# Spacing the rows of h 2112 bytes apart and the weight slots 4112 bytes apart in a one-core fp32 transformer kernel

## The chip, the core and the metric

The kernel runs on one NeuronCore of a Trainium2 chip. The core has a matrix engine (PE, with its own queue of weight loads, PEld), a vector engine (DVE), a scalar engine (ACT), a general engine (POOL) and a queue engine that only issues transfers (SP). Its on-chip memory (SBUF) has 128 partitions; a tensor such as `[128, 8, 512]` of fp32 lies in every partition as 8 rows of 512 numbers, 2048 bytes each, one behind the other. Matmul results go to a second memory, `ps`, of 8 banks per partition. The metric is device time in microseconds (us) of one execution of the whole program; lower is better.

## What is computed

A two-layer hybrid block for a latent diffusion model. There are 256 latent tokens and 256 context tokens (512 columns in the kernel), model width 1024. Each layer is a half-step SwiGLU, a token mixer and another half-step SwiGLU:

```
def ffn_sublayer(s, m, g_norm, w_in, w_out):
    h = modulate(rmsnorm(s, g_norm), m[0], m[1])
    return s + FFN_RES * m[2] * swiglu(h, w_in, w_out)

def mixer_sublayer(...):                       # cut
    h = modulate(rmsnorm(s, p["norm_mix"]), m[0], m[1])
    pool, qkv, z, ba, aq, ak, av, gate = split_cols(h @ p["w_in"])
    # multi-scale pooling | bidirectional gated DeltaNet (chunks of 64) | GQA with 2-D rotary
    m = ga * (y_pool @ wa) + gb * (y_dn @ wb) + gc * (y_att @ wc)
    x = x + mx[2] * (m @ w_out)
```

All in fp32. D_FF is 2816, so one SwiGLU multiplies by a 1024 x 5632 matrix and then a 2816 x 1024 one; the mixer's input projection is 1024 x 5136. The last mixer and the last SwiGLU need only the 256 latent tokens. The modulations come from SiLU(c) times a 1024 x 9216 matrix per layer, and a last RMSNorm gives the output.

## The kernel before

**Tiles and products.** Activations lie with channels on the partitions and tokens in the columns: `x[:, k, :]` is channel block k (128 channels) of all 512 tokens. The weights come in blocks of 128 output channels, `[128, 1024]` for a sum over eight channel blocks. To keep fp32 accuracy each operand is split into a rounded upper part and a rest, both in a one-pass fp32 format (`F32R`): `h` into `h_hi` and `h_lo`, a weight block into `w_hi` and `w_lo`. `products` (lines 2031 to 2037) issues three matmuls per pair of tiles: upper weights by upper rows, upper weights by lower rows, lower weights by upper rows. Each has its own weight load of 128 x 128 and streams 512 columns (both token halves), or 256.

**What the rows and slots are.** `h_hi` and `h_lo` hold the normed activations, eight rows k, written once per stage by ACT (`h_hi`) and DVE (`h_lo`) and then read by every matmul of the stage's first product. The hidden activations of a SwiGLU and the merged branches go to `a_hi` and `a_lo`, 22 rows of 512 numbers each. Weights go through a ring of four slots (`RING = 4`): a transfer lands in `raw[:, j, :]`, ACT rounds it to `w_hi[:, j, :]` (`cast`, line 825), and DVE subtracts (`lower`, line 1449) to give `w_lo[:, j, :]`. `raw` and `w_lo` are the same bytes: `raw` is allocated and released, and `w_lo` is placed over it. In the same way `gate_in` (24,576 bytes) lies over `h_hi` and the start of `h_lo`, and is used when h is done.

**Order.** The work is written out by hand per engine, with semaphores. SP issues the load of weight block b when the matmuls of block b - 4 are done (`load`, line 588); ACT casts when it has landed; DVE lowers when it is cast; PE waits for `s_lo` of that block. POOL issues the transfers of the modulation weights (`ada`), and DVE multiplies them in between (line 1481). The stages are SwiGLU, mixer, SwiGLU, SwiGLU, mixer, SwiGLU. In the long parts the loops have PE run block after block, 24 matmuls each.

**Where the tensors lie.** Within a partition they are placed one behind the other in the order of the declarations, each start rounded up to a multiple of 32 bytes. With the pad of 8 numbers ahead of it (`pad_rows`), `x` starts at a multiple of 2048 bytes, and so do, in turn, `h_hi`, `h_lo`, `raw`/`w_lo`, `w_hi`, `ada`, `buf_a`, `buf_b`, `a_hi` and `a_lo`. Hence every row of h and of a starts at a multiple of 2048 bytes and every weight tile of 128 numbers at a multiple of 512 bytes. The second half of a row (the context tokens) starts 1024 bytes behind. Not everything lies so: in the mixer `pre` takes 4160 bytes, so `conv`, `kT`, `pool_mats`, `prob` and others behind it start 64 bytes past a multiple of 2048.

Of the kernel before, what the change touches and what calls it, by code (L numbers as in the profile page):

```python
# [8 lines left out]
F32R = mybir.dt.float32r  # L9
# [4 lines left out]
P = 128  # L14
D = 1024
KD = D // P
LAT, CTX = 256, 256
TOK = LAT + CTX
# [23 lines left out]
MIX_STAGE = (1, 4)  # L42
STAGE_BASE = (FFN_BASE[0], MIX_BASE[0], FFN_BASE[1], FFN_BASE[2], MIX_BASE[1], FFN_BASE[3])
RING = 4
SPLIT_STAGES = (1, 2, 3, 4)
NORM_PARTS = (1, 2, 2, 2, 2, 1, 1)
SPLIT_OUT = 5
# [79 lines left out]
def build_program(nc, a):  # L127
    with ExitStack() as ctx:
        def sb(name, shape, dt=F32, at=ctx):
            return at.enter_context(nc.sbuf_tensor(name, shape, dt))  # L130
# [25 lines left out]
        x = sb("x", [P, KD, TOK])  # L156
        with ExitStack() as s:
            gate_in = sb("gate_in", [P, 4, 3, TOK], at=s)
        h_hi = sb("h_hi", [P, KD, TOK], F32R)
        h_lo = sb("h_lo", [P, KD, TOK], F32R)  # L160
        with ExitStack() as s:
            raw = sb("raw", [P, RING, KD * P], at=s)
        w_lo = sb("w_lo", [P, RING, KD * P], F32R)
        w_hi = sb("w_hi", [P, RING, KD * P], F32R)
        ada = sb("ada", [P, 2, KD * P])
        buf_a = sb("buf_a", [P, 2, TOK])
        buf_b = sb("buf_b", [P, 2, TOK])
# [55 lines left out]
        s = ExitStack()  # L223
# [16 lines left out]
        s = ExitStack()  # L240
# [98 lines left out]
        ps = ctx.enter_context(nc.psum_tensor("ps", [P, 8, 512], F32))  # L339
# [1615 lines left out]
        def _(pe):  # L1955
# [203 lines left out]
            def mixer_pe(l):  # L2159
# [12 lines left out]
                pe.wait_ge(bal.sem, bal.at(l, 1))  # L2172
                for k in range(KD):
                    wh, wl = ba_hi[:, k * P:(k + 1) * P], ba_lo[:, k * P:(k + 1) * P]
                    pe.matmul(ps[:, 6, :], wh, h_hi[:, k, :], start=(k == 0), stop=False)
                    pe.matmul(ps[:, 6, :], wh, h_lo[:, k, :], start=False, stop=False)
                    ins = pe.matmul(ps[:, 6, :], wl, h_hi[:, k, :], start=False, stop=(k == KD - 1))
                ins.then_inc(bap.sem, 1)
                for n in range(RING, N_PROJ):

# [3 lines left out]
                    if 9 <= n < 12:  # L2184
                        m = n - 2
                        pe.wait_ge(evac.sem, evac.at(l, m + 1))
                        for t in range((TOK if m == 7 else no) // P):
                            ins = pe.transpose(ps[:, m - 5, t * P:(t + 1) * P],
                                               channel_rows(m)[:, t * P:(t + 1) * P], ident)
                        ins.then_inc(tkt.sem, 1)  # L2190
                    if n == 6:
                        pe.wait_ge(bat.sem, bat.at(l, 1))
                        for t in range(TT):
                            ins = pe.transpose(ps[:, 6, t * 16:(t + 1) * 16], ba_rowsT[0:16, t * P:(t + 1) * P],
                                               ident[0:16, 0:16])
# [56 lines left out]
                for s in range(no // LAT):  # L2252
                    if s:
                        pe.wait_ge(pl2.sem, pl2.at(l, s))
                    for g in range(4):
                        r = slice((g % 2) * HD, (g % 2 + 1) * HD)
                        for kt in range(2):
                            ins = pe.matmul(ps[r, 4, (g // 2) * LAT:(g // 2 + 1) * LAT],
                                            pool_nat[:, 2 * s + kt, g * HD:(g + 1) * HD], pool_mats[:, kt, g, :],
                                            start=(kt == 0), stop=(kt == 1))  # L2260
# [5 lines left out]
                    for g in range(4):  # L2266
                        r = slice((g % 2) * HD, (g % 2 + 1) * HD)
                        ins = pe.matmul(ps[r, 5, (g // 2) * LAT:(g // 2 + 1) * LAT], w_pool[r, g // 2, :],
                                        pooled[r, s, g // 2, :], start=True, stop=True)
# [54 lines left out]
                for j in range(4):  # L2324
# [3 lines left out]
                    for t in range(TT):  # L2328
                        ins = pe.transpose(ps[:, j % 2, t * P:(t + 1) * P], src[:, t * P:(t + 1) * P], ident)
# [3 lines left out]
                for d in range(2):  # L2333
                    ins = pe.matmul(ps[:, 5, d * TT * 4:(d + 1) * TT * 4], tri(d), gdt[:, :, 4 * d:4 * d + 4],
                                    start=True, stop=True)
                for d in range(2):
                    ins = pe.matmul(ps[:, 5, 32 + d * TT * 4:32 + (d + 1) * TT * 4], ones[:, :], gdt[:, :, 4 * d:4 * d + 4],
                                    start=True, stop=True)
# [3 lines left out]
                for w in range(2):  # L2342
# [26 lines left out]
                    for t in (0, 2):  # L2369
                        for q in range(4):  # L2370
# [3 lines left out]
                            ins = pe.matmul(ps[:, 4 + q % 2, cols], qkvT[r, 2 + w, cols], qkvT[r, 2 + w, cols],  # L2374
                                            start=True, stop=True)
                            if l == 0 or t == 0:
                                ins = pe.matmul(ps[:, q % 2, cols], qkvT[r, 2 + w, cols], qkvT[r, w, cols],
                                                start=True, stop=True)
# [16 lines left out]
                    for i, b in enumerate(LEVELS):  # L2395
                        for h in range(2):
                            if i:
                                pe.wait_ge(tup.sem, tup.at(l, 2 * NL * w + 2 * (i - 1) + h + 1))
                            for d in range(2):
                                for q in range(4):  # L2400
                                    ins = pe.transpose(t_bank(d, h)[:, q, :], t_mat(d, 4 * h + q), ident)  # L2401
                            ins.then_inc(trp.sem, 1)
                            for q in range(4):
                                ins = pe.matmul(x_bank(h)[:, :, q, :].rearrange("p z (i c) -> p z i c", c=b),  # L2404
                                                amT[:, 4 * h + q, :], t_old(b, 4 * h + q, 1), start=True, stop=True)
                            ins.then_inc(xps.sem, 1)
                        for h in range(2):
# [3 lines left out]
                            for q in range(4):  # L2411
                                ins = pe.matmul(x_bank(h)[:, :, q, :], um[:, 4 * h + q, :], x_half(h)[:, :, q, :],  # L2412
                                                start=True, stop=True)
                            ins.then_inc(yps.sem, 1)
                    for h in range(2):
                        pe.wait_ge(tup.sem, tup.at(l, 2 * NL * (w + 1) - 1 + h))
                        for d in range(2):
                            for q in range(4):
                                ins = pe.transpose(t_bank(d, h)[:, q, :], t_mat(d, 4 * h + q), ident)
                            ins.then_inc(fin.sem, 1)  # L2420
                    for d in range(2):
                        pe.wait_ge(uev.sem, uev.at(l, 4 * w + 3 + d))
                        for q in range(8):
                            h = 2 * w + q % 2
                            ins = pe.matmul(ps[:, d, q * HD:(q + 1) * HD], u_mat(d)[:, q, :],
                                            vd_nat[:, q // 2, h * HD:(h + 1) * HD], start=True, stop=True)
                        ins.then_inc(ups.sem, 1)
                    pe.wait_ge(keg.sem, keg.at(l, w + 1))
                    for d in range(2):
                        for q in range(8):  # L2430
                            r = slice((q % 2) * HD, (q % 2 + 1) * HD)
                            ins = pe.matmul(ps[r, 2 + d, (q // 2) * P:(q // 2 + 1) * P], ke[:, 8 * d + q, :],
                                            u_mat(d)[:, q, :], start=True, stop=True)
# [232 lines left out]
```

## Time and profile before

| | |
|---|---|
| runs | 2300.62, 2301.11, 2306.16 us; median 2301.11 |
| profiled execution | 2311.86 us, of which 2310.2 us from the first to the last instruction (the span) |
| mean granted clock of PE | 0.975 of 2.4 GHz |
| PE busy | 2213.9 us, 96% of the span, 12654 matmuls |
| PE's weight loads | 1863.6 us, beside the matmuls |
| DVE busy | 1370.2 us, 59% |
| ACT busy | 885.3 us, 38% |
| POOL busy | 218.7 us, 9% |
| transfers | 303.86 MB, mean 132 GB/s |

An engine's busy time is the sum of its instructions' durations with overlaps counted once; a matmul's duration overlaps the next one's, since they are pipelined, so the pace of PE is read from the distances between starts, not from the durations. The profiled execution is 0.5% longer than the median of the runs; the three runs lie 5.5 us apart.

### The profile page before, as it was taken

Reading aid. Unit: us, or ns where it says so; the run is one execution under the profiler, and the core shown is the slowest. Engines: PE = TensorE matmul, PEld = TensorE weight load, DVE = VectorE, ACT = ScalarE, POOL = GpSimd, SP = SyncE. Lnnn points to the kernel's source line nnn. Section 1 sums busy time; section 2 is a strip of 40 time slices with the busy share of each in tenths; the row PEclk is TensorE's granted clock in tenths of the full one; section 3 lists DMA queues with packets and bytes.
Section 4 is the critical chain, followed back from the end, with each engine's and each line's share of the span. In section 5 each row is a group of like instructions: output and inputs, shape, how many; then the busy total and the mean of one; then the engine's idle time right before and its main releaser. Section 6 shows DMA issues by size and latency. Waiting matters only on the chain.

```text
span 2310.2 us, 33776 instructions
## 1 busy us (share of the span) xinstructions
PE 2213.9 (96%) x12654; PEld 1863.6 (81%) x12654; DVE 1370.2 (59%) x2301; ACT 885.3 (38%) x1375; POOL 218.7 (9%) x287
## 2 busy tenths in 40 slices
PE   6999999999999999999999999999999998898998
PEld 3788878987558777888888888888889777788998
DVE  4787876634456447478875356555356555665554
ACT  2433322533444325343222243332235543455553
POOL 0001022000001200300011100000210001001001
PEclk8999999999999989999999999999999999899999
DMA  6455554323012205345554334444343311144555
GB/s 261 146 197 185 197 182 135 133 82 93 31 42 69 70 27 200 109 164 191 199 189 130 95 121 148 138 153 130 106 130 118 109 46 49 66 163 146 182 173 155
DMA packets 96913, 303.86 MB, mean 132 GB/s; under 512 B 10673, under 2 KB 17329, under 8 KB 95921
## 3 DMA queue, kind: packets, MB, share of 16 engines
q1 hardware_dynamic: 77520, 232.96, 31.0%
q0 software_dynamic: 18720, 69.21, 8.9%
q8 instruction: 68, 1.11, 0.2%
q10 hardware_dynamic: 576, 0.34, 0.0%
q14 instruction: 29, 0.23, 0.0%
HBM read 291.99 MB, written 10.49 MB: 131 GB/s over the span
## 4 chain that ended last, share of the span: by engine, by line
PE 56%; DVE 4%; ACT 2%; issue 1%; DMA 1%; DVEq 0%; ACTq 0%; SPq 0%
PE ps L2035 17%; PE ps L2036 16%; PE ps L2037 16%; DVE w_lo L1449 1%; PE ps L2286 1%; PE ps L2307 1%; PE ps L2401 1%; PE ps L2473 1%; PE ps L2404 1%; PE ps L2471 1%; PE ps L2412 1%; PE ps L2223 0%; PE ps L2295 0%; ACT w_hi L825 0%; DMA raw<-in_w_up 0%
## 5 line engine op out<-in xcount | busy, mean ns | idle before, releaser
L2035 PE MATMUL ps<-h_hi,w_hi 128*128 128x512 f32 (+1 forms) x2176 | 779.9, 358 | 30.8 <-DVE w_lo L1449 12.7
L2036 PE MATMUL ps<-h_lo,w_hi 128*128 128x512 f32 (+1 forms) x2176 | 761.7, 350 | 0.0
L2037 PE MATMUL ps<-h_hi,w_lo 128*128 128x512 f32 (+1 forms) x2176 | 761.2, 350 | 0.0
L1449 DVE TENSOR_TENSOR w_lo<-raw,w_hi 128x1024 fp32r<-128x1024 f32 (+2 forms) x416 | 475.3, 1146 | 462.8 <-ACT w_hi L825 458.0
L825 ACT ACTIVATE w_hi<-raw 128x1024 fp32r<-128x1024 f32 (+2 forms) x416 | 404.6, 974 | 613.5 <-DMA raw<-in_w_down 306.7
L2035 PEld LDWEIGHTS ps<-h_hi,w_hi 128*128 128x128 f32 x2176 | 419.1, 193 | 121.1 <-issue 43.0
L2037 PEld LDWEIGHTS ps<-h_hi,w_lo 128*128 128x128 f32 x2176 | 419.1, 193 | 52.1
L2036 PEld LDWEIGHTS ps<-h_lo,w_hi 128*128 128x128 f32 x2176 | 419.7, 193 | 48.9
L2035 PE MATMUL ps<-a_hi,w_hi 128*128 128x512 f32 (+1 forms) x1050 | 359.4, 342 | 9.4 <-DVE buf_b L1912 3.7
L2036 PE MATMUL ps<-a_lo,w_hi 128*128 128x512 f32 (+1 forms) x1050 | 357.2, 340 | 0.0
L2037 PE MATMUL ps<-a_hi,w_lo 128*128 128x512 f32 (+1 forms) x1050 | 357.0, 340 | 0.0
L1481 DVE CUSTOM_DVE_ANT_0 ps<-ada,c_wide 128x1024 f32<-128x1024 f32 x256 | 319.2, 1247 | 6.8 <-DMA ada<-in_w_ada_t 1.6
L2035 PEld LDWEIGHTS ps<-a_hi,w_hi 128*128 128x128 f32 x1050 | 199.0, 189 | 35.7 <-DVE buf_b L1912 5.9
L2037 PEld LDWEIGHTS ps<-a_hi,w_lo 128*128 128x128 f32 x1050 | 199.0, 190 | 22.2
L2036 PEld LDWEIGHTS ps<-a_lo,w_hi 128*128 128x128 f32 x1050 | 199.1, 190 | 21.9
L723 POOL DMA_DIRECT2D ada<-in_w_ada_t x128 | 67.9, 531 | 804.1 <-DVE ada_sum L1481 797.2
L944 ACT ACTIVATE a_hi<-buf_b 128x512 f32 (+3 forms) x88 | 51.0, 579 | 201.3 <-DVE buf_b L1467 201.3
L1472 DVE TENSOR_TENSOR a_lo<-buf_b,a_hi 128x512 f32 (+3 forms) x88 | 54.7, 622 | 26.2 <-ACT a_hi L944 26.1
L685 POOL TENSOR_TENSOR buf_a<-x 128x512 f32<-128x512 f32 (+1 forms) x34 | 44.8, 1317 | 239.5 <-DVE x L1455 239.2
L1455 DVE SCALAR_TENSOR_TENSOR x<-ps,mod,x 128x256 f32<-128x256 f32 (+1 forms) x68 | 30.4, 479 | 53.6 <-PE ps L2037 53.6
L1467 DVE TENSOR_TENSOR buf_b<-buf_a,ps 128x512 f32<-128x512 f32 (+1 forms) x88 | 54.0, 614 | 8.4 <-PE ps L2037 8.4
L940 ACT ACTIVATE buf_a<-ps 128x512 f32<-128x512 f32 (+1 forms) x88 | 47.3, 537 | 14.2 <-PE ps L2037 13.8
(259 smaller groups left out, 1829.2 us busy)
## 6 DMA issues: line engine op xcount, KB each, us to landing
raw<-in_w_up SPq DMA_DIRECT2D x176, 512.0 KB, 3.7
ada<-in_w_ada_t POOLq DMA_DIRECT2D x128, 512.0 KB, 3.8
raw<-in_w_down SPq DMA_DIRECT2D x64, 384.0 KB, 3.1
raw<-in_w_gate SPq DMA_DIRECT2D x48, 512.0 KB, 3.5
raw<-in_w_down SPq DMA_DIRECT2D x64, 320.0 KB, 2.9
raw<-in_w_proj SPq DMA_DIRECT2D x32, 512.0 KB, 3.4
raw<-in_w_merge SPq DMA_DIRECT2D x16, 512.0 KB, 3.7
raw<-in_w_out SPq DMA_DIRECT2D x16, 512.0 KB, 3.3
```

The costliest lines, as they stand in the source:

```text
L685: link(pool.tensor_tensor(buf_a[:, 1, 0:n], xk, xk, ALU.mult))
L723: pool.dma_start(ada[:, j, :], a["w_ada_t"][ADA_FIRST - KD + 2 * r + j]).then_inc(s_ada[j], 16)
L825: return act.activation(w_hi[:, j % RING, 0:cols], raw[:, j, 0:cols], ACT.Copy)
L940: act.activation(buf_a[:, j, 0:n], ps[:, 2 * j, 0:n], ACT.Silu).then_inc(s_silu, 1)
L944: act.activation(a_hi[:, q, 0:n], buf_b[:, j, 0:n], ACT.Copy).then_inc(s_ahi, 1)
L1449: vec.tensor_tensor(w_lo[:, j % RING, 0:cols], raw[:, j, 0:cols], w_hi[:, j % RING, 0:cols].bitcast(F32), ALU.subtract).then_inc(s_lo, 1)
L1467: vec.tensor_tensor(buf_b[:, j, 0:n], buf_a[:, j, 0:n], ps[:, 2 * j + 1, 0:n], ALU.mult).then_inc(s_mul, 1)
L1472: vec.tensor_tensor(a_lo[:, q, 0:n], buf_b[:, j, 0:n], a_hi[:, q, 0:n].bitcast(F32), ALU.subtract).then_inc(s_alo, 1)
L1481: vec.tensor_tensor_reduce(ps[:, 6:8, :].rearrange("p b n -> p (b n)"), ada[:, j, :], c_wide[:, i, :], 1.0, 0.0, ALU.mult, ALU.add, ada_su ...
L2035: pe.matmul(out, wh, rows_hi[:, i, c], start=first, stop=False)
L2036: pe.matmul(out, wh, rows_lo[:, i, c], start=False, stop=False)
L2037: return pe.matmul(out, wl, rows_hi[:, i, c], start=False, stop=last)
```

## The change

Each row of `h_hi` and `h_lo` gets 16 unused numbers (64 bytes) behind its 512, and each ring slot of `raw`, `w_lo` and `w_hi` gets 4 unused numbers (16 bytes) behind its 1024. The three matmuls that took a whole row by `:` now name its 512 columns. Everything else is as it was, and every engine's list of instructions has the same operations on the same shapes in the same order; only addresses differ.

```
--- before.py
+++ after.py
@@ -42,6 +42,7 @@
 MIX_STAGE = (1, 4)
 STAGE_BASE = (FFN_BASE[0], MIX_BASE[0], FFN_BASE[1], FFN_BASE[2], MIX_BASE[1], FFN_BASE[3])
 RING = 4
+H_GAP, W_GAP = 16, 4
 SPLIT_STAGES = (1, 2, 3, 4)
 NORM_PARTS = (1, 2, 2, 2, 2, 1, 1)
 SPLIT_OUT = 5
@@ -156,12 +157,12 @@
         x = sb("x", [P, KD, TOK])
         with ExitStack() as s:
             gate_in = sb("gate_in", [P, 4, 3, TOK], at=s)
-        h_hi = sb("h_hi", [P, KD, TOK], F32R)
-        h_lo = sb("h_lo", [P, KD, TOK], F32R)
+        h_hi = sb("h_hi", [P, KD, TOK + H_GAP], F32R)
+        h_lo = sb("h_lo", [P, KD, TOK + H_GAP], F32R)
         with ExitStack() as s:
-            raw = sb("raw", [P, RING, KD * P], at=s)
-        w_lo = sb("w_lo", [P, RING, KD * P], F32R)
-        w_hi = sb("w_hi", [P, RING, KD * P], F32R)
+            raw = sb("raw", [P, RING, KD * P + W_GAP], at=s)
+        w_lo = sb("w_lo", [P, RING, KD * P + W_GAP], F32R)
+        w_hi = sb("w_hi", [P, RING, KD * P + W_GAP], F32R)
         ada = sb("ada", [P, 2, KD * P])
         buf_a = sb("buf_a", [P, 2, TOK])
         buf_b = sb("buf_b", [P, 2, TOK])
@@ -2172,9 +2173,9 @@
                 pe.wait_ge(bal.sem, bal.at(l, 1))
                 for k in range(KD):
                     wh, wl = ba_hi[:, k * P:(k + 1) * P], ba_lo[:, k * P:(k + 1) * P]
-                    pe.matmul(ps[:, 6, :], wh, h_hi[:, k, :], start=(k == 0), stop=False)
-                    pe.matmul(ps[:, 6, :], wh, h_lo[:, k, :], start=False, stop=False)
-                    ins = pe.matmul(ps[:, 6, :], wl, h_hi[:, k, :], start=False, stop=(k == KD - 1))
+                    pe.matmul(ps[:, 6, :], wh, h_hi[:, k, 0:TOK], start=(k == 0), stop=False)
+                    pe.matmul(ps[:, 6, :], wh, h_lo[:, k, 0:TOK], start=False, stop=False)
+                    ins = pe.matmul(ps[:, 6, :], wl, h_hi[:, k, 0:TOK], start=False, stop=(k == KD - 1))
                 ins.then_inc(bap.sem, 1)
                 for n in range(RING, N_PROJ):
```

What the addresses become, from the declarations (bytes within a partition, modulo 2048):

| tensor | start before | start after | its rows or slots after |
|---|---|---|---|
| x | 0 | 0 | unchanged |
| h_hi | 0 | 0 | row k at 64k |
| h_lo | 0 | 512 | row k at 512 + 64k |
| raw, w_lo | 0 | 1024 | slot j at 1024 + 16j |
| w_hi | 0 | 1088 | slot j at 1088 + 16j |
| ada, buf_a, buf_b, a_hi, a_lo | 0 | 1152 | rows and slots still 2048 or 4096 apart |
| what lies behind them | s | s + 1152 | distances among them unchanged |

The rows of `a_hi` and `a_lo` keep their spacing of 2048 bytes, but they too now start at another offset than the weight tiles that they are multiplied by. The tensors end 1152 bytes later and still fit.

## Rows read from the trace of the kernel before

**Rows 1.** The page: busy time by engine, the slices and the granted clock.

```profile
PE 2213.9 (96%) x12654; PEld 1863.6 (81%) x12654; DVE 1370.2 (59%) x2301; ACT 885.3 (38%) x1375; POOL 218.7 (9%) x287
PE   6999999999999999999999999999999998898998
PEclk8999999999999989999999999999999999899999
```

**Rows 2.** PE's waits by what released it: in total, times, longest.

```profile
PE ps L2401 <- ACT tm L1213: 19.1, 4, 8.4
PE ps L2035 <- DVE w_lo L1449: 15.8, 14, 4.4
PE ps L2035 <- DVE h_lo L1357: 9.8, 6, 3.4
PE ps L2035 <- DVE h_lo L1409: 6.0, 5, 1.5
```

**Rows 3.** PE in order of time, 512 columns, rows of h: start, duration.

```profile
1099.79 0.39 PE L2035 MATMUL ps<-h_hi,w_hi 128*128 128x512 f32 x1
1100.02 0.39 PE L2036 MATMUL ps<-h_lo,w_hi 128*128 128x512 f32 x1
...
1105.91 0.39 PE L2035 MATMUL ps<-h_hi,w_hi 128*128 128x512 f32 x1
```

**Rows 4.** The same, 512 columns, rows of a.

```profile
300.57 0.39 PE L2035 MATMUL ps<-a_hi,w_hi 128*128 128x512 f32 x1
...
303.97 0.39 PE L2035 MATMUL ps<-a_hi,w_hi 128*128 128x512 f32 x1
```

**Rows 5.** The same, 256 columns, rows of h, last SwiGLU.

```profile
2149.77 0.28 PE L2036 MATMUL ps<-h_lo,w_hi 128*128 128x256 f32 x1
...
2153.13 0.28 PE L2037 MATMUL ps<-h_hi,w_lo 128*128 128x256 f32 x1
```

**Rows 6.** Costliest groups with shapes apart: busy us, mean ns, idle before.

```profile
L2036 PE MATMUL ps<-h_lo,w_hi 128*128 128x512 f32 x1296 | 507.5, 392 | 0.0
L2036 PEld LDWEIGHTS ps<-h_lo,w_hi 128*128 128x128 f32 x2176 | 419.7, 193 | 48.9
L1449 DVE TENSOR_TENSOR w_lo<-raw,w_hi 128x1024 fp32r<-128x1024 f32 x288 | 353.5, 1229 | 301.3 <-ACT w_hi L825 297.2 <-DVE mod_rest L1486 2.2
L825 ACT ACTIVATE w_hi<-raw 128x1024 fp32r<-128x1024 f32 x288 | 303.2, 1055 | 306.8 <-DMA raw<-in_w_up 275.9 <-DMA raw<-in_w_out 28.2 <-DMA raw<-in_w_merge 2.1
L2036 PE MATMUL ps<-a_lo,w_hi 128*128 128x512 f32 x566 | 220.3, 389 | 0.0
L2036 PEld LDWEIGHTS ps<-a_lo,w_hi 128*128 128x128 f32 x1050 | 199.1, 190 | 21.9
```

**Rows 7.** Two stretches, engines busy (instructions), clock, DMA share, GB/s.

```profile
1360.00:1540.00 180.00, 180.00 (x859) 151.79 (x858) 107.16 (x154) 72.46 (x90) 8.47 (x16) 1.00 0.44 143
2150.00:2300.00 150.00, 150.00 (x1251) 149.90 (x1250) 81.06 (x100) 73.58 (x99) 11.50 (x13) 1.00 0.57 174
```

**Rows 8.** Transfers, whole span: count, KB each, median us to landing.

```profile
raw<-in_w_up SPq DMA_DIRECT2D x176, 512.0 KB, 3.7
masks<-in_consts SPq DMA_DIRECT2D x2, 1024.0 KB, 5.7
pool_mats<-in_pool_mats SPq DMA_DIRECT2D x2, 1024.0 KB, 4.9
```

**Rows 9.** Transfers, from 2050 to 2300 us.

```profile
raw<-in_w_up SPq DMA_DIRECT2D x44, 512.0 KB, 3.3
```

More of the change, by code:

```diff
@@ L44 @@
 RING = 4
+H_GAP, W_GAP = 16, 4
 SPLIT_STAGES = (1, 2, 3, 4)
@@ L158, in build_program @@
             gate_in = sb("gate_in", [P, 4, 3, TOK], at=s)
-        h_hi = sb("h_hi", [P, KD, TOK], F32R)
-        h_lo = sb("h_lo", [P, KD, TOK], F32R)
+        h_hi = sb("h_hi", [P, KD, TOK + H_GAP], F32R)
+        h_lo = sb("h_lo", [P, KD, TOK + H_GAP], F32R)
         with ExitStack() as s:
-            raw = sb("raw", [P, RING, KD * P], at=s)
-        w_lo = sb("w_lo", [P, RING, KD * P], F32R)
-        w_hi = sb("w_hi", [P, RING, KD * P], F32R)
+            raw = sb("raw", [P, RING, KD * P + W_GAP], at=s)
+        w_lo = sb("w_lo", [P, RING, KD * P + W_GAP], F32R)
+        w_hi = sb("w_hi", [P, RING, KD * P + W_GAP], F32R)
         ada = sb("ada", [P, 2, KD * P])
@@ L2174, in mixer_pe @@
                     wh, wl = ba_hi[:, k * P:(k + 1) * P], ba_lo[:, k * P:(k + 1) * P]
-                    pe.matmul(ps[:, 6, :], wh, h_hi[:, k, :], start=(k == 0), stop=False)
-                    pe.matmul(ps[:, 6, :], wh, h_lo[:, k, :], start=False, stop=False)
-                    ins = pe.matmul(ps[:, 6, :], wl, h_hi[:, k, :], start=False, stop=(k == KD - 1))
+                    pe.matmul(ps[:, 6, :], wh, h_hi[:, k, 0:TOK], start=(k == 0), stop=False)
+                    pe.matmul(ps[:, 6, :], wh, h_lo[:, k, 0:TOK], start=False, stop=False)
+                    ins = pe.matmul(ps[:, 6, :], wl, h_hi[:, k, 0:TOK], start=False, stop=(k == KD - 1))
                 ins.then_inc(bap.sem, 1)
```

## The prediction

> **What bounds the kernel now.** I read the page first: PE is busy 96% of the span and every other engine under 60%, and the digits of PE stand at 9 nearly throughout [rows 1]. So the kernel is worth what PE's pace is worth, plus the little that PE waits. The view of waits comes second: what PE waits for weights and rows of h is 15.8 + 9.8 + 6.0 = 31.6 us in 25 waits, 1.4% of the span, and the largest single item has nothing to do with them [rows 2]. Third come the starts of PE's matmuls in order of time, since durations overlap and don't give a pace.
>
> With 512 columns and rows of h, 27 steps take 1105.91 - 1099.79 = 6.12 us, 226.7 ns each [rows 3]. With 256 columns, 28 steps take 2153.13 - 2149.77 = 3.36 us, 120.0 ns each [rows 5]. The difference, 106.7 ns for 256 columns, is 0.417 ns a column, 2.4 GHz. What is left is fixed: 226.7 - 512 x 0.417 = 13.3 ns for every matmul, whatever its length. The granted clock is 1.00 in the second of these stretches [rows 7]. This fixed part is the only place in PE's steady pace where a better layout could find something.
>
> **Is the fixed part a matter of addresses?** If reading a row of h next to a weight tile collided, the price should depend on where they lie to each other, or on how long they are read together. The two lengths have the same 13.3 ns. The steps of one window run over all k, with weight tiles 512 bytes apart against rows 2048 bytes apart, so that the distance modulo 1024 and 2048 changes from k to k, and the starts keep their beat of 0.22 to 0.23 us. The rows of a, another tensor elsewhere, show 15 steps in 303.97 - 300.57 = 3.40 us, again 226.7 ns [rows 4]. A collision that goes by 1024 or 2048 bytes is therefore excluded. One that goes by 512 bytes or less is not: before the change all of these operands start at multiples of 512, and after it hardly any pair does. No row of this trace shows an F32R matmul off that grid, so both ends must be kept. I take the value zero, because a constant that holds for three settings is most simply the cost of changing the weights: each of these matmuls has its own weight load [rows 6].
>
> **Part by part.**
>
> PE. The matmuls of `products` are 2176 x 3 with rows of h and 1050 x 3 with rows of a, 9678 in all (the counts of weight loads in [rows 6] are 2176 and 1050 for one of the three). At best all of the fixed part goes: 9678 x 13.3 ns = 129 us. For the other end the nearest row is the mean duration, 392 ns with h and 389 with a at 512 columns [rows 6]: 3 ns is the largest difference between two tensors that the trace shows, and if the changed offsets cost that much per matmul it is 9678 x 3 ns = 29 us. I take 0.
>
> ACT's casts. 288 of 1055 ns and shorter ones, 416 in all; DVE's lower, 288 of 1229 ns [rows 6]. Their operands now start 16, 32 or 48 bytes past the old grid. All numbers stay 4 bytes wide and contiguous. The cover is ample: in the stretch of 1360 to 1540 us ACT is busy 72.46 and DVE 107.16 of 180 us while PE has not one gap [rows 7], and in 2150 to 2300 us the figures are 73.58 and 81.06 of 150. It fails only where PE does wait for `w_lo`, 14 times [rows 2]: if a cast and a lower both became 10% dearer, that is 14 x 0.1 x (1.055 + 1.229) = 3.2 us, and as much gained if they became cheaper. I take 0.
>
> Writing h. ACT and DVE write a row of h in one piece, as before; only its start moves. PE's waits there are 15.8 us [rows 2], and 10% of that is 1.6 us. I take 0.
>
> Transfers. A weight block is 128 rows of 4096 bytes. Before, each landed at a multiple of 2048; now slots 1 to 3 start 16, 32 and 48 bytes off a multiple of 64. The trace has one natural comparison: `masks` and `pool_mats` are the same size, 8192 bytes a partition; `masks` starts on a multiple of 512 and `pool_mats` 64 bytes off it. They land in 5.7 and 4.9 us [rows 8], so 64 bytes off costs nothing. For 16 bytes there is no row. Suppose such packets took twice as long. In the last SwiGLU 174 GB/s go at a share of 0.57, so the full rate is 305 GB/s and a block of 512 KB (524,288 bytes) takes 1.7 us of all 16 engines; doubling adds 1.7 us to a landing of 3.3 [rows 9]. A ring slot comes round every 4 x 24 x 0.120 = 11.5 us there; in it lie its own 2.9 us of matmuls, 3.3 of landing, 1.06 of cast and 1.23 of lower, 8.5 in all. 3.0 us of slack swallow the 1.7. With 512 columns the round is 21.8 us. So I take 0 here too; beyond a doubling see the third rival.
>
> Instructions, waits and queues are the same in number and order, so no wait is added and none is moved. The sum is 0: against the profiled execution 2311.86 us, which lies 10.75 us above the median of the runs it is compared with; I carry the zero to that median, 2301.11 us.
>
> **A rule of the skill against the change.** The rows above have PE untouched by what ACT, DVE and the transfers do: 180 of 180 us busy with DVE at 107 and DMA at 0.44 [rows 7]. The Trainium skill's page "SBUF — State Buffer", section "Who interferes with whom", says that contention exists only at the port pair shared by DVE and GpSimd, and that PE and ACT never wait on anyone. By that rule no spacing within a partition can gain or lose anything, the sum stays zero; the trace agrees as far as the rows go.
>
> **Rivals.**
>
> First, faster: the fixed 13.3 ns are, wholly or partly, a collision of row and weight tile that start on the same 512-byte grid, and shifting them by 64 and 16 bytes dissolves it. For it: the constant is there, and it is paid 9678 times. Against it: it does not vary at all. Whole, it gives 2301 - 129 = 2172 us; a quarter gives 2269. It passes what can be measured from 6.9 us / 9678 = 0.7 ns per matmul, less than two cycles. The Trainium skill's "TensorE: Matmul & The Clock Gate", section "Wait — 56ns, not 53.3ns?", has a fixed cost of about 2.5 ns for matmuls back to back; were the rest of our 13.3 avoidable, 9678 x 10.8 ns = 105 us would go, to 2196 us. The trace's 13.3 ns disagrees with that figure, but there each matmul does not bring new weights, so I give it little.
>
> Second, slower: the common start was the good one. Seven rows of eight, and all of a against the weights, now start at mixed offsets, and each start costs PE something, at 3 ns [rows 6] 29 us: 2330 us. For it: all tensors before the change start on one grid, and the trace has nothing else. Against it: fixed cost and column rate look like clock cycles, not like memory lines. It decides from 0.7 ns as well.
>
> Third, slower: packets to slots that are off by 16 bytes take over twice as long. In the last SwiGLU, three slots of four at f times the price give a share of 0.57 x (0.25 + 0.75 f), which reaches 1 at f = 2.0. At f = 2.5 it is 1.21, and the roughly 200 us of that stage become 42 us longer: 2343 us. For it: no row has such a start. Against it: 64 bytes off is free.
>
> Fourth, the change doesn't do what its numbers say: a, a third of the products, keeps its 2048 bytes, and 16 bytes between slots is a small shift. That ends at my forecast's time.
>
> **Numbers.** Within 0.3% (6.9 us, 2294.2 to 2308.0) a measurement of this kernel can't tell a change from none; the three runs spread over 5.5 us. Nothing changes, the fourth rival included: 0.72, of which 0.63 is measured as the same, 0.05 as faster and 0.04 as slower, since the short stretches at the lower clock (the digits 8 of PEclk in [rows 1]) need not fall alike. First rival 0.15, mostly a small part of it; second 0.08; third 0.05. So faster 0.20, same 0.63, slower 0.17. The predicted time is 2301 us. The range from 2286 to 2315 holds the forecast and the small sizes of either rival and leaves out their large ones.
>
> **What would show it.** Right: starts of F32R matmuls still 226.7 and 120.0 ns apart, for h and for a; casts at 1055 and lowers at 1229 ns within 1%; landings of 3.7 and 3.3 us. First rival: the distances fall below 226 and 119 ns, in h alone or in a too. Second: they rise, or begin to depend on k. Third: the landing of weight blocks rises above 5 us, the DMA share of the last stage goes to 0.9, and PE's line there shows gaps with ACT waiting for `raw`. My forecast is wrong if PE's pace moves by 1 ns or more, or if a new wait of PE for `w_lo` adds up to over 7 us.

## The result, and the profile after

| | before | after |
|---|---|---|
| runs, us | 2300.62, 2301.11, 2306.16 | 2314.64, 2317.50, 2320.24 |
| median, us | 2301.11 | 2317.50 |
| ratio to before | | 1.0064, 95% interval 1.0035 to 1.0093 |
| profiled execution, us | 2311.86 | 2314.64 |
| mean granted clock in it | 0.975 | 0.984 |

The change costs 16.4 us by the medians, 8 to 21 us by the interval. The forecast was 2301 us, the same, with a range to 2315. It was wrong: the kernel became slower, and the time lies 2.5 us above the range.

The two profiled executions differ by 2.8 us only, because the one of before had more time at the lower clock. What that is worth can be read from the 15 runs of the kernel before that were taken beside e2_rows_only: over mean clocks of 0.975 to 0.984 their time falls by about 1.7 us for each 0.001. The 0.009 between the two profiled executions are then some 15 us, and at one clock they lie about 18 us apart (an estimate).

The page of the kernel after, the busy times and the granted clock, against [rows 1]:

```profile
PE 2216.6 (96%) x12654; PEld 1846.6 (80%) x12654; DVE 1370.2 (59%) x2301; ACT 885.9 (38%) x1375; POOL 219.8 (10%) x287
PEclk8999999999999999999999999999999999899999
```

PE is busy 2.7 us longer although it had the higher clock, and the others did the same work in the same time. The lines of the source are one higher from here on (L2036 to L2038 for `products`).

Kernel after, what PE waits for (total, times, longest), against [rows 2]:

```profile
PE ps L2402 <- ACT tm L1214: 18.6, 4, 8.4
PE ps L2036 <- DVE w_lo L1450: 16.6, 14, 4.4
PE ps L2036 <- DVE h_lo L1358: 8.9, 6, 3.4
PE ps L2036 <- DVE h_lo L1410: 6.0, 5, 1.4
```

The three waits for weights and rows of h add up to 31.5 us; they were 31.6. PE doesn't wait more. Next its starts, in the window of [rows 3] (512 columns, rows of h):

```profile
1100.08 0.40 PE L2037 MATMUL ps<-h_lo,w_hi 128*128 128x512 f32 x1
1100.31 0.39 PE L2038 MATMUL ps<-h_hi,w_lo 128*128 128x512 f32 x1
...
1101.23 0.40 PE L2036 MATMUL ps<-h_hi,w_hi 128*128 128x512 f32 x1
1101.47 0.39 PE L2037 MATMUL ps<-h_lo,w_hi 128*128 128x512 f32 x1
1101.69 0.39 PE L2038 MATMUL ps<-h_hi,w_lo 128*128 128x512 f32 x1
...
1106.32 0.40 PE L2037 MATMUL ps<-h_lo,w_hi 128*128 128x512 f32 x1
```

27 steps take 1106.32 - 1100.08 = 6.24 us, 231.1 ns each, where they took 226.7. The beat is uneven now: 0.23, then 0.24, then 0.22 us. Rows of a, against [rows 4], and 256 columns, against [rows 5]:

```profile
302.93 0.39 PE L2036 MATMUL ps<-a_hi,w_hi 128*128 128x512 f32 x1
...
306.87 0.40 PE L2038 MATMUL ps<-a_hi,w_lo 128*128 128x512 f32 x1
...
2149.76 0.28 PE L2037 MATMUL ps<-h_lo,w_hi 128*128 128x256 f32 x1
...
2153.07 0.28 PE L2038 MATMUL ps<-h_hi,w_lo 128*128 128x256 f32 x1
```

With a, 17 steps take 3.94 us, 231.8 ns each. With 256 columns 28 steps take 3.31 us: 118.2 ns, which is less than the 120.0 of before. So one length got slower and the other faster. The groups say the same, against [rows 6]:

```profile
L2037 PE MATMUL ps<-h_lo,w_hi 128*128 128x512 f32 x1296 | 510.8, 394 | 0.0
L2037 PEld LDWEIGHTS ps<-h_lo,w_hi 128*128 128x128 f32 x2176 | 412.9, 190 | 54.1
L1450 DVE TENSOR_TENSOR w_lo<-raw,w_hi 128x1024 fp32r<-128x1024 f32 x288 | 353.2, 1228 | 309.3 <-ACT w_hi L826 305.4 <-DVE mod_rest L1487 2.2
L826 ACT ACTIVATE w_hi<-raw 128x1024 fp32r<-128x1024 f32 x288 | 303.2, 1055 | 317.3 <-DMA raw<-in_w_up 284.5 <-DMA raw<-in_w_out 28.2 <-DMA raw<-in_w_merge 3.6
L2037 PE MATMUL ps<-a_lo,w_hi 128*128 128x512 f32 x566 | 224.1, 396 | 0.0
```

The cast stands at 1055 ns and the lower at 1228 (1229 before): here operands that start 16, 32 or 48 bytes off cost ACT and DVE nothing. The transfers, whole span and then 2050 to 2300 us, against [rows 8, 9]:

```profile
raw<-in_w_up SPq DMA_DIRECT2D x176, 512.0 KB, 3.9
ada<-in_w_ada_t POOLq DMA_DIRECT2D x128, 512.0 KB, 3.7
```

```profile
raw<-in_w_up SPq DMA_DIRECT2D x44, 512.0 KB, 3.3
```

The landing is 3.9 us against 3.7 over the span, and 3.3 as before in the last SwiGLU. The 0.2 us don't come from the 16 bytes: e2_rows_only, whose slots keep their 4096 bytes, has 4.3 us in both, and e3_slots_only, with the 16 bytes alone, 3.8 and 3.2. What moves the landings is open; PE's wait for `w_lo` is 15.1 and 15.5 us there, no more than before.

**The account.** These are the mean distances from one F32R start to the next over the whole trace, in ns, worked out from the starts of single matmuls of one kind. Distances over 260 ns (512 columns) or 140 ns (256) are left out, so that waits and stretches at the lower clock don't count:

| kernel | 512, h | 512, a | 256, h | 256, a |
|---|---|---|---|---|
| before | 227.1 | 226.8 | 119.8 | 119.9 |
| after | 231.6 | 231.9 | 118.2 | 117.4 |

The 9678 matmuls of `products` are 3888 and 1698 with 512 columns, 2640 and 1452 with 256. 5586 x 4.7 = +26 us, 4092 x 1.9 = -8 us: +18 us together. That is close to the difference of the medians (16.4) and to the 18 us between the profiled executions at one clock.

Two more things stand in the single starts. Before, 92% of the distances with 512 columns and h are 226 or 227 ns (3419 of 3701); after, 98% of them spread from 225 to 239. And each distance of after belongs to its place in the order of the matmuls, which repeats every four blocks, 96 matmuls: the 8 to 10 repetitions of one place in one stretch scatter by 0.4 ns (standard deviation; the trace counts whole ns), whatever ACT, DVE and the transfers do then.

### The profile page after: what moved, and what is told of

The parts are those of the page before. It is cut to its first block, busy times and chain, and to the rows that moved or that the text cites. A ratio compares the mean times of both kernels' runs of the same rounds, so it can differ in the third digit from the quotient of the medians.

```text
span 2312.9 us, 33776 instructions
## 1 busy us (share of the span) xinstructions
PE 2216.6 (96%) x12654; PEld 1846.6 (80%) x12654; DVE 1370.2 (59%) x2301; ACT 885.9 (38%) x1375; POOL 219.8 (10%) x287
## 4 chain that ended last, share of the span: by engine, by line
PE 55%; DVE 4%; ACT 2%; issue 1%; DMA 1%; DVEq 0%; ACTq 0%; SPq 0%
PE ps L2036 16%; PE ps L2037 16%; PE ps L2038 16%; DVE w_lo L1450 1%; PE ps L2287 1%; PE ps L2308 1%; PE ps L2402 1%; PE ps L2405 1%; PE ps L2413 1%; PE ps L2224 0%; PE ps L2296 0%; PE ps L2474 0%; PE ps L2472 0%; DMA raw<-in_w_up 0%; ACT w_hi L826 0%
## 5 line engine op out<-in xcount | busy, mean ns | idle before, releaser
L2036 PE MATMUL ps<-h_hi,w_hi 128*128 128x512 f32 (+1 forms) x2176 | 778.0, 358 | 30.7 <-DVE w_lo L1450 13.2
L2038 PE MATMUL ps<-h_hi,w_lo 128*128 128x512 f32 (+1 forms) x2176 | 761.0, 350 | 0.0
L2036 PEld LDWEIGHTS ps<-h_hi,w_hi 128*128 128x128 f32 x2176 | 412.9, 190 | 125.3 <-issue 42.0
L2038 PEld LDWEIGHTS ps<-h_hi,w_lo 128*128 128x128 f32 x2176 | 413.1, 190 | 57.3
L2037 PEld LDWEIGHTS ps<-h_lo,w_hi 128*128 128x128 f32 x2176 | 412.9, 190 | 54.1
L2036 PE MATMUL ps<-a_hi,w_hi 128*128 128x512 f32 (+1 forms) x1050 | 362.0, 345 | 9.7 <-DVE buf_b L1913 4.1
L2038 PE MATMUL ps<-a_hi,w_lo 128*128 128x512 f32 (+1 forms) x1050 | 358.7, 342 | 0.0
L2036 PEld LDWEIGHTS ps<-a_hi,w_hi 128*128 128x128 f32 x1050 | 198.3, 189 | 39.1 <-DVE buf_b L1913 5.4
L2038 PEld LDWEIGHTS ps<-a_hi,w_lo 128*128 128x128 f32 x1050 | 198.5, 189 | 25.0
```

The source lines that it names most:

```text
L2036: pe.matmul(out, wh, rows_hi[:, i, c], start=first, stop=False)
L2037: pe.matmul(out, wh, rows_lo[:, i, c], start=False, stop=False)
L2038: return pe.matmul(out, wl, rows_hi[:, i, c], start=False, stop=last)
```

## The experiments

My theory after the result: while a matmul streams a row, the next weight tile is read beside it, and where the two lie to each other sets the price. The rival: other engines or transfers disturb PE through the new offsets. A second question was how fine the grid is, and which of the two gaps matters.

**e1_pairs: PE alone.** A kernel that isn't the block: two casts fill `rows` and `weights`, then PE runs 196 settings of 8 matmuls while nothing else works (the loop, shortened).

```
+for i, (n, m, w, step) in enumerate(cases()):      # n columns; m, w: starts in numbers of 4 bytes
+    for r in range(8):
+        at = w + step * r
+        pe.matmul(ps[:, i % 4, 0:n], weights[:, at:at + P], rows[:, m:m + n], start=True, stop=True)
```

> This is not the block but a measurement of PE by itself: 196 settings, each 8 matmuls in a row with one weight load each (F32R, 128 x 128 weights, 512 or 256 columns), with the row starting m numbers and the weight tile w numbers past a multiple of 2048 bytes; no other engine works beside it and its output is not the block's. The profile after has matmuls of 512 columns at 231.4 ns on average, scattered between 224 and 239, where before had 226.7 throughout. Theory 1 (the price of a matmul depends on where row and weight tile lie relative to each other): 226.7 and 120.0 ns for m = w = 0 and whenever m = w (d = 4, 8, 16, 32, 64), something else, between 224 and 239 ns, for m = 16 with w = 0 and the same for m = 0 with w = -16. Rival (each operand's own start counts, off a grid it costs extra): m = w = 4 or 16 is as dear as the two single shifts together. Second rival (the scatter comes from the other engines' reads and writes at the new addresses, not from PE's own two reads): with PE alone all 196 settings show 226.7 and 120.0 ns.

The page of this kernel:

```profile
PE 276.9 (93%) x1572; PEld 242.1 (81%) x1572; ACT 10.3 (3%) x5; POOL 0.2 (0%) x4
```

ACT's five operations lie outside the 196 settings. Yet with rows and weights both at 0, PE takes 226.7 ns (512 columns) and 120.0 (256), the beat of the kernel before, and with rows 16, 128 or 192 bytes off it takes 232.7, 233.3 and 233.3 with 512 columns, where the kernel after has 231.6 on average. A weight tile 256 bytes on gives 226.7 again. So the second rival, the other engines, falls: two operands of PE are enough. With 256 columns and a row 192 bytes on it goes down to 113.3 to 114.0. The first rival, each operand's own start, would have made two shifts add up: 16 bytes of the row alone give 232.7 and 16 bytes of the weights alone 233.3, so both together some 239; they gave 230.0. In one place my theory was too simple: rows and weights shifted by the same amount did not all go back to 226.7 (64 bytes: 226.7; but 16 bytes: 230.0; 128: 231.5). Eight matmuls are short, and the rhythm that a setting settles into can hang on the one before. That doesn't explain the 16 bytes, where 232 and 228 ns alternate steadily.

**e6_fine: the curve.** The same with ten matmuls per setting, row starts in steps of 4 bytes against four starts of the weights (the list of settings, shortened).

```
+for n in (512, 256):
+    for w in (0, 16, 32, 48):
+        for m in range(64): out.append((n, m, w))
```

> PE alone again (not the block, its output is not the block's), 10 matmuls per setting: rows starting 0 to 252 bytes off in steps of 4, weight tiles at 0, 64, 128 and 192, for 512 and 256 columns. Theory 1 (only the distance modulo 256 counts): the four weight starts give the same curve shifted by 64 bytes each, with 226.7 ns at distance 0 as one of the lowest of 512 columns, and 113.3 at -64 as the lowest of 256 columns. Rival (the start of the row or of the weights by itself counts): the curves differ in shape. If some distance shows less than 226.7 ns at 512 columns (220 ns, 16 cycles beside the columns as at 256, would be the next one), a better layout for long matmuls exists as well.

PE in order of time (a row is one setting of ten: start, from the first start to the last end). Weights at 64 bytes; rows at 52, 56, 60, 64, 68 and 72 bytes, 512 columns:

```profile
198.20 2.56 PE L72 MATMUL ps<-rows,weights 128*128 128x512 f32 x10
200.59 2.47 PE L70 MATMUL ps<-rows,weights 128*128 128x512 f32 x10
202.90 2.44 PE L72 MATMUL ps<-rows,weights 128*128 128x512 f32 x10
205.18 2.44 PE L70 MATMUL ps<-rows,weights 128*128 128x512 f32 x10
207.46 2.52 PE L72 MATMUL ps<-rows,weights 128*128 128x512 f32 x10
209.82 2.49 PE L70 MATMUL ps<-rows,weights 128*128 128x512 f32 x10
```

The starts lie 2.39, 2.31, 2.28, 2.28 and 2.36 us apart for ten matmuls. Four bytes turn 228 ns into 236. Settled (the last six distances of a setting) they are 240.0, 230.0, 227.5, 226.7 at equal starts, and 236.7. The same weights with 256 columns, rows at 76, 80 and 84 and then at 168 and 172 bytes:

```profile
714.45 1.33 PE L72 MATMUL ps<-rows,weights 128*128 128x256 f32 x10
715.62 1.29 PE L70 MATMUL ps<-rows,weights 128*128 128x256 f32 x10
716.75 1.38 PE L72 MATMUL ps<-rows,weights 128*128 128x256 f32 x10
...
741.81 1.45 PE L70 MATMUL ps<-rows,weights 128*128 128x256 f32 x10
743.10 1.36 PE L72 MATMUL ps<-rows,weights 128*128 128x256 f32 x10
```

1.17 us, then 1.13 (rows 16 bytes past the weights, settled 113.3 ns), and 1.29 at the dear end (104 bytes past, settled 130.0). The four weight starts give the same curve, moved by their 64 bytes: 117 of the 128 points agree within 1 ns. So for weights on multiples of 64 bytes the distance counts, modulo 256 bytes, and not where either lies; for weights in between, as the kernel after has them, the 230.0 ns of e1_pairs leaves that open. Settled values in ns (the middle of the four weight starts), by how many bytes the row starts past the weights:

| past by | 0 | 16 | 32 | 48 | 64 | 80 | 96 | 112 |
|---|---|---|---|---|---|---|---|---|
| 512 | 226.7 | 230.7 | 233.2 | 232.8 | 228.8 | 231.2 | 233.3 | 231.2 |
| 256 | 118.8 | 113.3 | 116.7 | 118.5 | 117.8 | 119.8 | 120.0 | 117.7 |

| past by | 128 | 144 | 160 | 176 | 192 | 208 | 224 | 240 |
|---|---|---|---|---|---|---|---|---|
| 512 | 233.3 | 233.0 | 234.5 | 233.3 | 233.3 | 234.5 | 233.3 | 236.7 |
| 256 | 120.0 | 113.3 | 117.7 | 119.0 | 114.2 | 119.3 | 117.8 | 117.3 |

No distance goes under 226.7 with 512 columns: equal starts are the floor there, shared with 28, 60 and 156 bytes, and the mean of all 64 distances is 233.1. With 256 columns equal starts are ordinary: 118.8 here, 120.0 in the kernel, where the mean of all 64 is 119.1. So an arbitrary shift costs the long matmuls some 6 ns on average and leaves the short ones about where they were.

A value of this table isn't fixed by the distance alone. Rows 240 bytes past the weights settled at 236.7 here, after a setting of 236 bytes, and at 226.7 in e1_pairs, after one of 224. With 256 columns, 16 bytes past gave 113.3 in the table and 119.0 at the end of the same run, after equal starts. The pairs are the same; what differs is what came before them. The four sweeps of e6_fine say the same: each distance follows the one 4 bytes smaller in all of them, except at the start of a sweep, and the 11 points that don't agree all lie in the first seven settings of one (192 bytes with 256 columns: 117.8 ns as the first of a sweep, 114.2 in the other three).

The table comes near the kernel after. Its starts modulo 256 bytes are 64k for the rows of h, 16j for `w_lo`, 64 + 16j for `w_hi` and 128 for a. The pairs of h fall on all sixteen columns alike: the means are 232.5 and 117.6 ns, and the kernel has 231.6 and 118.2. Those of a lie 16 to 64 past `w_hi` (two thirds of them) and 80 to 128 past `w_lo`: 231.7 and 117.5, and the kernel has 231.9 and 117.4. Before, everything stood in the first column. These are means; e4_shift_only below shows that single steps don't follow the table.

**e2_rows_only and e3_slots_only: each gap alone.**

```
-H_GAP, W_GAP = 16, 4
+H_GAP, W_GAP = 16, 0      # e2_rows_only
+H_GAP, W_GAP = 0, 4       # e3_slots_only
```

> Rows of h 2112 bytes apart, ring slots at 4096 as before. h_lo, the slots and a stay on a grid of 256 bytes to each other, only rows of h lie at 64k against the weights. Theory 1 (the price of a matmul is set by the distance, modulo 256 bytes, between the row it streams and the weight tile that is loaded beside it; PE alone showed with 512 columns 226.7 to 228.3 ns at distance 0, 228.8 to 230.8 at 64, about 233.3 at 128 and 192; with 256 columns about 120, 118, 118 and 113.8): products with rows of h average 230.9 ns at 512 columns and 117.4 at 256, those with a stay at 226.7 and 120.0. That is 3888 x 4.2 - 2640 x 2.6 = +9.5 us, 2311 us. Rival 2 (rows 2048 bytes apart matter in themselves, whatever the weights do): the whole 16 us of the change, 2317. Rival 3 (the slots' 16 bytes do it, by the transfers or the casts): 2301.

> Ring slots 4112 bytes apart, rows of h at 2048. Now w_hi starts 64 and a 128 bytes off the grid of w_lo's first slot, and slot j 16j more. Theory 1, with the prices that PE alone showed at these distances: h on average 232.5 ns at 512 columns and 118 at 256, a 232.2 and 118.1: (3888 x 5.8 + 1698 x 5.5) - (2640 x 2.0 + 1452 x 1.9) = +24 us, 2325 us, more than the change itself. Rival 2 (the rows matter in themselves): 2301. Rival 3 (the slots do it by transfers or casts): 2317, with landings of over 3.9 us or casts over 1060 ns and PE's paces still 226.7 and 120.0.

e2_rows_only: 2315.39 us, 1.0057 [1.0032, 1.0082]. e3_slots_only: 2317.94 us, 1.0084 [1.0057, 1.0112]. Groups of e2_rows_only:

```profile
L2037 PE MATMUL ps<-h_lo,w_hi 128*128 128x512 f32 x1296 | 513.6, 396 | 0.0
L2037 PE MATMUL ps<-a_lo,w_hi 128*128 128x512 f32 x566 | 220.3, 389 | 0.0
```

and of e3_slots_only:

```profile
L2037 PE MATMUL ps<-h_lo,w_hi 128*128 128x512 f32 x1296 | 511.5, 395 | 0.0
L2037 PE MATMUL ps<-a_lo,w_hi 128*128 128x512 f32 x566 | 223.4, 395 | 0.0
```

With the rows alone spaced, weights and a stay on one grid: a keeps its 389 ns and its 226.9 between starts, only h moves (231.7). With the slots alone spaced, h and a both move (232.0). Each half costs about what the whole does: once a pair is off the good distance, a second shift has nothing more to spoil. My numbers for both were off: 2311 for the rows, which came to 2315 (h at 231.7 and 118.1 ns, where I had 230.9 and 117.4), and 2325 for the slots, which came to 2318 (h at 232.0, where I had 232.5, and a at 232.0 and 117.4).

**e4_shift_only: the starts without the gaps.** Rows 2048 and slots 4096 bytes apart, the tensors' starts as in the kernel after.

```
         h_hi = sb("h_hi", [P, KD, TOK], F32R)
+        sb("pad_h", [P, 128])
         h_lo = sb("h_lo", [P, KD, TOK], F32R)
+        sb("pad_w", [P, 128])
         ...                                   # cut: raw, on the bytes of w_lo
         w_lo = sb("w_lo", [P, RING, KD * P], F32R)
+        sb("pad_wh", [P, 16])
         w_hi = sb("w_hi", [P, RING, KD * P], F32R)
+        sb("pad_ada", [P, 16])
```

> Nothing is spaced wider: rows 2048 and slots 4096 bytes apart as before, but pads of 512, 512, 64 and 64 bytes put h_lo, the slots, w_hi and everything behind at the very starts that they have after the change. Theory 1: the spacing as such is not needed for the loss. h against w_hi lies at 192 modulo 256, h_lo against w_lo at 0, a at 64 and 128: h averages 231.1 ns at 512 columns and 115.7 at 256, a 231.0 and 118: +24.5 us from 512 columns and -14.3 from 256 columns, 2311 us. A pace of about 113.5 ns must appear for two of three products with h at 256 columns. Rival 2 (rows or slots at a power of two, or not, are what counts): 2301 and 226.7 and 120.0 ns throughout.

2318.92 us, 1.0076 [1.0048, 1.0104]. I had 2311. The spacing that the change is named for isn't needed: shifting the starts of whole tensors costs as much. Starts are 232.0 ns apart with h and 233.1 with a, where I had 231.1 and 231.0. The 256-column rows of a are at 116.2 (118), and those of h, which I had at 113.5 for two of three products, at 118.0 throughout: here each row stands 192 past `w_hi` but 0 past `w_lo`, so the distance changes from one matmul to the next. That this mixing is what keeps it from 113.5 is my reading; no run isolates it, but e8_shift_all, with 192 for all pairs, has 114.7.

Single steps don't follow the table once distances are mixed. The starts of e4_shift_only, 512 columns:

```profile
1099.92 0.39 PE L2039 MATMUL ps<-h_hi,w_hi 128*128 128x512 f32 x1
1100.14 0.40 PE L2040 MATMUL ps<-h_lo,w_hi 128*128 128x512 f32 x1
1100.38 0.39 PE L2041 MATMUL ps<-h_hi,w_lo 128*128 128x512 f32 x1
1100.61 0.39 PE L2039 MATMUL ps<-h_hi,w_hi 128*128 128x512 f32 x1
```

To the ns these three steps are 226, 236 and 232, and so they repeat in this window. The first two pairs stand 192 bytes past and the third 0, where the table has 233.3, 233.3 and 226.7. The mean of the three, 231.3, agrees with the table's 231.1, but the share of each matmul doesn't, nor does it if each row is taken with the next weight tile in place of its own. So the table gives means, and for mixed distances only roughly: 231.1 ns would be the mean for all of e4_shift_only's h, which has 232.0, and 230.3 for its a, which has 233.1.

**e5_slots_256: a gap of the grid's own size.**

```
+H_GAP, W_GAP = 0, 64      # slots 4352 bytes apart, 17 x 256
```

> Ring slots 4352 bytes apart (a gap of 256 bytes), rows of h at 2048. Theory 1 with a grid of 256 bytes: all distances stay 0 modulo 256, so the paces stay 226.7 and 120.0 ns and the time 2301 us, although no slot is a power of two behind the other any more. Rival (a coarser grid, 512 bytes or more, is what counts; slots 1 and 3 are 256 bytes off it): half of the products move to 228 to 233 ns, +8 to +15 us.

2302.33 us, 1.0008 [0.9988, 1.0027]: no change. The starts of e5_slots_256, 512 and 256 columns:

```profile
1099.75 0.39 PE L2036 MATMUL ps<-h_hi,w_hi 128*128 128x512 f32 x1
...
1105.87 0.39 PE L2036 MATMUL ps<-h_hi,w_hi 128*128 128x512 f32 x1
...
2149.78 0.28 PE L2038 MATMUL ps<-h_hi,w_lo 128*128 128x256 f32 x1
...
2153.14 0.28 PE L2036 MATMUL ps<-h_hi,w_hi 128*128 128x256 f32 x1
```

6.12 us for 27 steps and 3.36 for 28, to the hundredth what [rows 3, 5] have. Moving slots by a multiple of 256 bytes costs nothing here.

**e8_shift_all: every weight block 64 bytes into its slot.** With slots of 4352 bytes there is room for it, and all rows now stand 192 past all weights.

```
+def start(b):
+    return W_SHIFT        # 16 numbers
-                sp.dma_start(raw[:, j, 0:cols], src).then_inc(s_raw[j], 16)
+                o = start(b if like is None else like)
+                sp.dma_start(raw[:, j, o:o + cols], src).then_inc(s_raw[j], 16)
```

The cast, the lower and `products` take the same `o`.

> The same, but with every weight block 64 bytes into its slot, those of 512 columns too. Theory 1: 512 columns go to 233.3 ns (5586 x 6.6 = +37 us), 256 columns to 113.3 ns (4092 x 6.5 = -27 us, or -8 in the slower rhythm): 2311 us, up to 2330. Rival (what counts is that rows and slots are not at the same power of two): 2301.

2318.21 us, 1.0078 [1.0051, 1.0105]. Its starts:

```profile
1099.65 0.40 PE L2048 MATMUL ps<-h_hi,w_lo 128*128 128x512 f32 x1
...
1105.96 0.39 PE L2048 MATMUL ps<-h_hi,w_lo 128*128 128x512 f32 x1
```

27 steps take 6.31 us, 233.7 ns; the mean over the trace is 233.2 with h and 233.3 with a, where the table has 233.3 for 192. With 256 columns the means are 114.7 and 115.5, against 114.2. It is the purest test of the curve in the block, one distance for all pairs, and it holds for both lengths with opposite signs: 5586 x 6.3 = +35 us, and 2640 x 5.1 + 1452 x 4.4 = -20 us. The sum of +15 us compares with 17.9 by the ratio of the times.

**e7_short_shift: each length at its own good distance.** The same code, but `start(b)` is 16 numbers only for blocks that meet 256-column products alone, and 0 otherwise.

```
+def start(b):
+    for f in range(4):
+        if 0 <= b - FFN_BASE[f] < N_FFN:
+            return W_SHIFT if f == 3 or (f and b - FFN_BASE[f] < RING) else 0
+    if b >= MIX_BASE[1]:
+        return 0 if b - MIX_BASE[1] in (6, 7) else W_SHIFT
+    n = b - MIX_BASE[0]
+    return W_SHIFT if n < RING or n >= BRANCH_BLOCK + KD + SPLIT_OUT else 0
```

> Rows of h at 2048 and ring slots 4352 bytes apart (as in the run of slots 256 bytes apart), and every weight block whose products have only 256 columns is put 64 bytes into its slot: 3696 of the 4092 matmuls of 256 columns; all 5586 of 512 columns stay at distance 0. Theory 1: 226.7 ns stays at 512 columns; at 256 columns the distance -64 modulo 256 settled at 113.3 ns with PE alone (once at 117.8, where another start of the sequence was given): 3696 x 6.5 ns = 24 us less at best, 2277 us, and 8 us less, 2293, if the slower of the two rhythms is met. Rival (the gain seen with PE alone is lost with other engines at work or with mixed instructions between): 120 ns and 2301 us.

2293.36 us (12 runs) against 2302.1 (17 of before), 0.9961 [0.9944, 0.9977]: it beats both kernels. Its span, its busy times and two of its waits from the page and the waits:

```profile
span 2281.8 us, 33734 instructions
PE 2179.9 (96%) x12654; PEld 1834.5 (80%) x12654; DVE 1369.9 (60%) x2301; ACT 884.9 (39%) x1375; POOL 219.7 (10%) x287
```

```profile
PE ps L2419 <- ACT tm L1228: 20.2, 4, 8.4
PE ps L2052 <- DVE w_lo L1465: 18.2, 17, 4.6
```

and its starts in the last SwiGLU:

```profile
2149.76 0.28 PE L2052 MATMUL ps<-h_hi,w_hi 128*128 128x256 f32 x1
...
2152.94 0.28 PE L2053 MATMUL ps<-h_lo,w_hi 128*128 128x256 f32 x1
```

28 steps in 3.18 us, 113.6 ns, where [rows 5] have 120.0. 512 columns stay at 227.1 and 226.8. By the means over the trace (114.4 and 116.4) 2640 x 5.4 + 1452 x 3.4 = 19 us should go. Of these, 6 come back as idle time of PE (2281.8 - 2179.9 = 101.9 us without work, 2310.2 - 2213.9 = 96.3 before). Part of it is that with shorter products PE waits 17 times for `w_lo` and not 14, 18.2 us and not 15.8. That leaves 13. The runs show 9: at a mean clock of 0.980 the kernel before takes about 2302.2 us and this one 2293.5 (lines through the 17 and the 12 runs, each falling by 1.7 us for 0.001). The two fastest, 2283.48 and 2279.68 us at 0.985 and 0.986, lie some 11 below the line of before. What takes the rest is open.

My 2293 for "the slower of the two rhythms" was met by luck: PE runs mostly in the faster one (77% of the steps with h at 256 columns are 113 or 114 ns), which I had priced at 2277.

All kernels side by side: mean steps in ns, worked out as in the account, what they add up to against before, and the measured ratio times 2301 us.

| kernel | 512, h | 512, a | 256, h | 256, a | sum, us | measured, us |
|---|---|---|---|---|---|---|
| before | 227.1 | 226.8 | 119.8 | 119.9 | | |
| after | 231.6 | 231.9 | 118.2 | 117.4 | +18 | +15 (8 to 21) |
| e2_rows_only | 231.7 | 226.9 | 118.1 | 119.9 | +14 | +13 (7 to 19) |
| e3_slots_only | 232.0 | 232.0 | 118.1 | 117.4 | +20 | +19 (13 to 26) |
| e4_shift_only | 232.0 | 233.1 | 118.0 | 116.2 | +20 | +17 (11 to 24) |
| e5_slots_256 | 227.1 | 226.8 | 119.8 | 119.9 | 0 | +2 (-3 to 6) |
| e8_shift_all | 233.3 | 233.3 | 114.7 | 115.5 | +15 | +18 (12 to 24) |
| e7_short_shift | 227.1 | 226.8 | 114.4 | 116.4 | -19 | -9 (-13 to -5) |

PE's steps account for every one of the slower kernels within the interval; for e7_short_shift they promise twice what came.

## Why the prediction was wrong

**The step that failed** is the one headed by the question whether the fixed part is a matter of addresses: "I take the value zero, because a constant that holds for three settings is most simply the cost of changing the weights". The three settings were not three: the distances that varied in them were all multiples of 256 bytes, so they were one setting seen three times [rows 3 to 5]. The same step had said that no row shows a pair off the 512-byte grid, and then let the constant speak for the region it hadn't seen. Against the zero the runs show +4.7 ns a matmul with 512 columns and -1.9 with 256, +18 us in the sum; and e1_pairs and e6_fine show the address dependence itself, with PE alone.

**The fixed part.** 13.3 ns is not one constant. With 512 columns it is a floor, which e6_fine found no distance to go under. With 256 columns it falls to 113.3 - 106.7 = 6.6 ns. The two lengths agreed at 13.3 because the chosen distance is the best for one and a middling one for the other. And at its best neither length shows a fixed part: 226.7 ns is twice 113.3, 544 and 272 cycles of 2.4 GHz, 17 cycles for every 16 columns. Two lengths can't tell more than that.

**The second rival was right** in its mechanism, at 0.08 the second least of my chances: "the common start was the good one". Its size was taken as 3 ns on every matmul, 29 us; it is 4.7 ns on 58% of them and a gain on the rest, 18 us. The 3 ns themselves, 392 against 389 in [rows 6], said nothing of addresses: the steps of the two at the full clock are 227.1 and 226.8. My argument against it, that the fixed cost looks like clock cycles and not like memory lines, doesn't exclude memory: settled values such as 226.7, 233.3 and 240.0 ns are 544, 560 and 576 cycles of 2.4 GHz, and which of them comes goes by address. The first rival expected the collision where the starts are equal. There a shift helps the 256 columns alone, by 8 us.

**PE's two reads.** I wrote that by the Trainium skill's "SBUF — State Buffer", section "Who interferes with whom", no spacing within a partition can gain or lose anything. As for other engines it stands: e1_pairs gives the beats of the kernel before with PE alone. But that section goes engine by engine, and I took its rule to settle PE's two reads against each other as well. The Trainium skill's "TensorE: Matmul & The Clock Gate", section "Step-by-step: what each phase is for", does speak of them: "Loading the next tile's weights doesn't steal SBUF read bandwidth from the running matmul." Here the measurement decides otherwise: with nothing changed but the distance of the two, a matmul of 512 columns takes from 226.7 to 240.0 ns (e6_fine).

**What held.** Casts 1055 ns, lowers 1228, landings 3.3 us in the last stage (3.9 and not 3.7 over the span), and PE's waits at 31.5 us: the zeros for ACT, DVE, the writing of h, and the transfers were right, and the third rival is gone. The fourth, that the shifts are too small or miss a, was wrong twice: 4 bytes are enough (e6_fine), and a, which keeps its own spacing, is off its old distance to the weights (e3_slots_only).

**The range.** The upper end of 2315 came from small sizes of a rival whose own price was 2330. With the bounds of -129 and +29 us worked out and no row between them, the middle of the second rival belonged inside.

What stays open is the cause inside the chip. The runs show that the mean price goes by the distance modulo 256 bytes, differently for each length, and that single steps depend on the matmuls before; not what is being shared, nor how the matmuls before come in.

## What to carry to other kernels

Where each F32R matmul brings its own weights, the start of the streamed row against the start of the weight tile is a tuning knob, of up to 13 ns a matmul with PE alone and some 6 in these kernels. Choose it per number of columns (here equal modulo 256 bytes for 512 columns, 192 bytes past for 256), give all pairs of one length the same distance, and measure it with PE alone in one small kernel first, in the order in which the kernel will issue the matmuls. A pad between tensors or rows that isn't a multiple of 256 bytes changes it unasked. A constant seen in several rows is evidence only for what varied in them: list what stayed the same in all before taking a value outside.

## What the runs showed of the hardware

- The start-to-start time of F32R matmuls with new weights each depends on where row and weight tile lie to each other: 226.7 to 240.0 ns for 512 columns and 113.3 to 130.0 for 256, by distance modulo 256 bytes (weights on multiples of 64), with steps of 4 bytes telling (e6_fine: 227.5, 226.7, 236.7 at -4, 0 and +4).
- The best distance isn't the same for the two lengths, and one of 192 costs 6 ns at 512 columns while it gains 5 at 256 (e8_shift_all).
- The same distance can settle at two values, by what came before: 240 bytes past at 226.7 (e1_pairs) and 236.7 ns (e6_fine). With mixed distances single steps don't follow the curve: 226, 236 and 232 ns in e4_shift_only.
- A step at the same place of the repeating order is steady to 0.4 ns in a kernel with all engines and transfers at work.
- ACT, DVE and transfers didn't notice starts 16 bytes off: 1055 ns, 1228 ns, and 3.3 us for a block of 512 KB.
